# Key products of the cache scores: GpSimd alone, or GpSimd and VectorE in pairs of chunks

## The reference

```
h = rmsnorm(x);  proj = h @ w_in           # 1024 -> 2824: conv, gating, q, k, v, forget logits
logf = log_sigmoid(f + b_f)
prompt: causal attention over 512 tokens, 8 heads of 64, logits + sum of logf
sample: s_past = (q . k_past) * 64**-0.5 + logf + suffix sums of the cached logf
        p = softmax([s_past, s_new]);  o = p @ [v_past, v]
x = x + concat(rmsnorm of the three mixers) @ w_o
x = x + mixture of 32 experts (top 1 group, top 2 in it);  x = x + (p @ w_ple) * sigmoid(...)
```

## Time and profile before

| | us |
|---|---|
| median of three runs | 1118.66 (1113.89 to 1123.4) |
| the profiled execution, its own time | 1116.41 |
| its span | 1114.6 |
| PE busy / DVE busy / ACT busy / POOL busy | 894.7 / 322.5 / 192.6 / 315.8 |
| key products on POOL (L662) x32 | 145.1 |
| key reductions on DVE (L1743) x32 | 72.9 |
| mean granted clock of PE | 0.889 |

### The profile page before, as it was taken

One profiled execution on the slowest core, in us unless ns is written; L12 is line 12 of the kernel. 1 busy time (PEld: TensorE's weight loads), 2 busy tenths in 40 slices (PEclk: granted clock), 3 DMA queues, 4 the chain that ended last, 5 costly groups with the idle time before them and its releaser, 6 DMA issues.

```text
span 1114.6 us, 11569 instructions
## 1 busy us (share of the span) xinstructions
PE 894.7 (80%) x4270; PEld 464.2 (42%) x4270; DVE 322.5 (29%) x710; ACT 192.6 (17%) x388; POOL 315.8 (28%) x336
## 2 busy tenths in 40 slices
PE   2899929998878868767988788778788787886796
PEld 2488716675753424433333333233233333332342
DVE  5217455776464213453100000000000000000562
ACT  2010114554400000211110110110111011100332
POOL 5637899891002231002111111110111111001110
PEclk9899968998869799888998898899889889988799
DMA  9146676662604898640999999999999999998310
GB/s 310 45 151 225 225 253 213 223 226 110 247 1 166 339 376 328 255 179 21 359 413 409 400 412 395 409 414 402 412 416 410 400 411 404 424 401 340 154 40 38
DMA packets 53688, 316.42 MB, mean 284 GB/s; under 512 B 11103, under 2 KB 23967, under 8 KB 32905
## 3 DMA queue, kind: packets, MB, share of 16 engines
q1 hardware_dynamic: 30720, 232.43, 52.1%
q0 software_dynamic: 14512, 76.17, 18.9%
q10 hardware_dynamic: 8416, 7.30, 2.1%
HBM read 309.31 MB, written 14.82 MB: 291 GB/s over the span
## 4 chain that ended last, share of the span: by engine, by line
PE 38%; DMA 36%; POOL 13%; DVE 7%; issue 3%; ACT 2%; SPq 1%; POOLq 0%; DVEq 0%; ACTq 0%
DMA arena<-in_w_up 28%; PE psum L1572 12%; POOL arena L662 9%; PE psum L1680 5%; DMA arena<-in_cache_v,indices 5%; PE psum L1424 4%; PE psum L1277 3%; PE psum L1203 3%; POOL arena L615 2%; DMA arena<-in_w_down 2%; PE psum L1343 2%; DVE arena L1743 1%; POOL arena L593 1%; PE psum L1528 1%; PE psum L1365 1%
## 5 line engine op out<-in xcount | busy, mean ns | idle before, releaser
L1572 PE MATMUL psum<-arena 128*64 128x512 f32 x1024 | 271.6, 691 | 80.7 <-DMA arena<-in_w_up 80.7
L1572 PEld LDWEIGHTS psum<-arena 128*64 128x64 f32 x1024 | 90.7, 158 | 237.5 <-issue 235.4
L662 POOL TENSOR_TENSOR arena<-arena 128x2048 f32<-128x2048 f32 x32 | 145.1, 4535 | 3.6 <-ACTq L824 3.0
L2178 DVE TENSOR_TENSOR arena<-arena,psum 64x512 f32<-64x512 f32 x32 | 22.1, 692 | 382.1 <-ACT arena L1060 382.1
L1587 PE MATMUL psum<-arena 128*64 128x512 f32 x512 | 118.7, 605 | 4.2 <-DMA arena<-in_w_down 3.6
L692 POOL COPY indices<-row_list 128x1 int32 (+1 forms) x26 | 4.7, 181 | 306.0 <-ACT arena L1066 306.0
L1743 DVE TENSOR_REDUCE arena<-arena 128x32 f32<-128x2048 f32 x32 | 72.9, 2283 | 57.3 <-POOL arena L662 57.0
L1203 PE MATMUL psum<-arena 128*128 128x260 f32 x384 | 84.6, 383 | 0.7 <-ACT arena L827 0.7
L1277 PE MATMUL psum<-arena 128*128 128x260 f32 x320 | 79.3, 402 | 0.0
L1203 PEld LDWEIGHTS psum<-arena 128*128 128x128 f32 x384 | 72.8, 190 | 12.3 <-ACT arena L827 1.2
L1060 ACT ACTIVATE arena<-psum 64x512 f32<-64x512 f32 x32 | 18.8, 588 | 332.7 <-PE psum L1572 332.7
(11 more groups left out here) (318 smaller groups left out, 862.6 us busy)
## 6 DMA issues: line engine op xcount, KB each, us to landing
arena<-in_w_down SPq DMA_DIRECT2D x32, 2048.0 KB, 25.1
arena<-in_w_gate SPq DMA_DIRECT2D x31, 2048.0 KB, 18.2
arena<-in_w_up SPq DMA_DIRECT2D x31, 2048.0 KB, 22.6
arena<-in_w_in SPq DMA_DIRECT2D x11, 1024.0 KB
arena<-in_x_prompt SPq DMA_DIRECT2D x8, 512.0 KB, 6.7
arena<-in_w_o SPq DMA_DIRECT2D x1, 4096.0 KB, 14.0
arena<-in_w_ple_gate SPq DMA_DIRECT2D x1, 4096.0 KB, 26.4
arena<-moe_rows SPq DMA_DIRECT2D x4, 1024.0 KB, 7.8
```

What stands on the lines that cost most here:

```text
L662: pool.tensor_tensor(r, r, q_rep, ALU.mult).then_inc(kmul, 1)
L1572: last = mm(bank(s)[m * SLOTS:(m + 1) * SLOTS, :], hgT[s][:, k, :], w_gu[s][m][:, k, :], start=(k == 0), stop=(k == DC - 1))
```

## The change

- **Pairs.** The first 24 key chunks (`SHARED`) are worked in pairs: GpSimd multiplies the even chunk, VectorE the odd one, and VectorE reduces both. VectorE reads the query from PSUM bank 6, where PE leaves it (`qb` is no fill any more). The last eight chunks stay with GpSimd, and their reductions stand in steps 1 to 6 of the attention (`REDUCE_AT`).
- **Six slots.** The ring has six slots for the first 24 chunks; two lie over the normalised rows and the input rows, whose first use afterwards waits for reduction 24. GpSimd issues four gathers ahead of its constants, two after them, and from then on two per pair, two pairs ahead.
- **Forget gate.** PE transposes the forget logits behind the first projected tile, not the fourth; VectorE works the gate in three parts behind pairs 1, 2 and 3, and some of its operands are in PSUM bank 7. ACT's Exp and Ln stand behind the second and the third copy of a projected tile.
- **Scans.** The eight scans stand ahead of the sum of the query's halves.
- **Value copies.** v0 and v1 behind pair 9, v2 and v3 behind pair 10; then pair 11.
- Semaphores are shared or renumbered in the value and expert stages, with constants added to their waits.

```diff
+SHARED = 24
+V_AFTER = {9: (0, 1), 10: (2, 3)}
+REDUCE_AT = {24: (1, 0), 25: (1, 1), 26: (2, 1), 27: (3, 0), 28: (3, 1), 29: (4, 1), 30: (5, 1), 31: (6, 0)}
+SLOT = [n % 6 if n < SHARED else n % 4 for n in range(CHUNKS)] + [n % 4 for n in range(CHUNKS)]
+def arrived(n):
+    return 16 * (1 + SLOT[:n].count(SLOT[n]))
...
-        ring = [at(region_b + s * CW, CW) for s in range(4)]
+        ring = [at(region_b + s * CW, CW) for s in range(4)] + [at(xn0, CW), at(x0, CW)]
-        f_a, f_b, f_c, f_d = (small(TILES, HC) for _ in range(4))
+        f_a, f_c, f_d = (psum[:, 7, n * TILES * HC:(n + 1) * TILES * HC].rearrange("p (t h) -> p t h", h=HC) for n in range(3))
+        f_b, f_e, f_g = (small(TILES, HC) for _ in range(3))
... GpSimd
-            for s in range(3):
-                load_chunk(0, s)
+            for n in range(4):
+                load_chunk(0, n)
...
+            for half in "ab":
+                pool.wait_ge(free_of(f"x{QT}{half}"), AT[f"x{QT}{half}"][1] + 1)
+            load_chunk(0, 4)
+            load_chunk(0, 5)
             pool.wait_ge(qb_ready, 1)
...
-            for n in range(CHUNKS):
-                products(n % 4, 16 * (n // 4 + 1))
-
-                pool.wait_ge(kred, n + 1)
-                if n + 3 < CHUNKS:
-                    load_chunk(0, n + 3)
-                else:
-                    load_chunk(1, n + 3 - CHUNKS)
+            for n in range(0, SHARED, 2):
+                products(n)
+                if n:
+                    pool.wait_ge(kred, n)
+                    load_chunk(0, n + 4)
+                    load_chunk(0, n + 5)
+            for n in range(SHARED, CHUNKS):
+                products(n)
+                if n > SHARED:
+                    pool.wait_ge(kred, n)
+                    load_chunk((n + 3) // CHUNKS, (n + 3) % CHUNKS)
... ScalarE
-            wait_full(act, "qb")
-            act.activation(q_bc, fill("qb"), ACT.Copy).then_inc(free_of("qb"), 1)
-            act.wait_ge(free_of("qb"), AT["qb"][1] + 1)
-            act.nop().then_inc(qb_ready, 1)
+            act.wait_ge(qb_full, 1)
+            act.activation(q_bc, bank(6), ACT.Copy).then_inc(qb_ready, 1)
...
+                if q == 1:
+                    act.wait_ge(f_part, 1)
+                    act.activation(f_b, f_a, ACT.Exp, scale=-1.0).then_inc(f_part, 1)
+                if q == 2:
+                    act.wait_ge(f_part, 3)
+                    act.activation(f_d, f_c, ACT.Ln).then_inc(f_part, 1)
... TensorE
-            pe.wait_ge(f_free, 1)
-            for s in range(2):
-                for q in range(2):
-                    project(s, q, 16, None if s == 0 else q + 1)
...
+            project(0, 0, 16, None)
             wait_free(pe, "f")
+            pe.wait_ge(f_free, 1)
             for t in range(TILES):
...
             done(last, "f")
+            project(0, 1, 16, None)
+            for q in range(2):
+                project(1, q, 16, q + 1)
... VectorE
+            dve.wait_ge(lf_in, 16)
+            for h in range(HC):
+                step(v.tensor_tensor_scan(decay[:, :, h], ones, logf_pages[:, :, h], 0.0, ALU.mult, ALU.add))
+            tell(suf_ready)
             dve.wait_ge(free_of("qs"), AT["qs"][1] + 1)
             v.tensor_tensor(q_s[0:NB, :], q_parts[0:NB, 0, :], q_parts[0:NB, 1, :], ALU.add).then_inc(qs_ready, 1)
...
+            def reduce_keys(n):
+                if n >= SHARED:
+                    dve.wait_ge(kmul, SHARED // 2 + n - SHARED + 1)
+                elif n % 2 == 0:
+                    dve.wait_ge(kmul, n // 2 + 1)
+                v.tensor_reduce(scores[:, n * KEYS * HC:(n + 1) * KEYS * HC], ring[SLOT[n]].rearrange("p (a d) -> p a d", d=HD),
+                                AX.X, ALU.add).then_inc(kred, 1)
+            q_rep = bank(6).rearrange("p (o n) -> p o n", o=1).to_broadcast([P, KEYS, WC])
+            def key_pair(n):
+                dve.wait_ge(kv_in[SLOT[2 * n + 1]], arrived(2 * n + 1))
+                r = ring[SLOT[2 * n + 1]].rearrange("p (k n) -> p k n", k=KEYS)
+                step(v.tensor_tensor(r, r, q_rep, ALU.mult))
+                reduce_keys(2 * n)
+                reduce_keys(2 * n + 1)
...
+            dve.wait_ge(qb_ready, 1)
+            key_pair(0)
+            key_pair(1)
+            forget_in()
+            key_pair(2)
+            forget_exp()
+            key_pair(3)
+            forget_log()
+            key_pair(4)
+            mask_ws()
+            for n in range(5, SHARED // 2):
+                key_pair(n)
+                for t in V_AFTER.get(n, ()):
+                    copy_values(t)
```

More of the change, by code:

```diff
@@ L78 @@
 FILLS = (["params"] + [f"x{t}{s}" for t in range(TILES) for s in "ab"]
-         + ["qs", "qb", "f", "ws", "ks", "vs", "ct"] + [f"{n}{t}" for t in range(QT) for n in "kv"]
+         + ["qs", "f", "ws", "ks", "vs", "ct"] + [f"{n}{t}" for t in range(QT) for n in "kv"]
          + ["suffix"]
@@ L1185, in _ @@
                 if s:
-                    wait_free(pe, "qb")
                     pe.wait_ge(qs_ready, 1)
                     pe.wait_ge(consts_built, 2)
-                    done(mm(fill("qb"), row_sel[0:NB, :], q_s[0:NB, :], start=True, stop=True), "qb")
+                    mm(bank(6), row_sel[0:NB, :], q_s[0:NB, :], start=True, stop=True).then_inc(qb_full, 1)
                 for k in range(DC):
@@ L1748, in _ @@
+            tell(suf_ready)
             dve.wait_ge(free_of("qs"), AT["qs"][1] + 1)
             v.tensor_tensor(q_s[0:NB, :], q_parts[0:NB, 0, :], q_parts[0:NB, 1, :], ALU.add).then_inc(qs_ready, 1)
-            for j in range(2):
-                reduce_static(j)
-            wait_full(dve, "f")
-            dve.wait_ge(consts_in, 16 * 15)
-            step(v.tensor_tensor(f_nat[:, 0:QT, :], fill("f")[:, 0:QT * HC].rearrange("p (t h) -> p t h", h=HC), outer(bf_bc, QT), ALU.add))
-            step(v.tensor_tensor(f_nat[0:NB, QT, :], fill("f")[0:NB, QT * HC:TILES * HC], bf_bc[0:NB, :], ALU.add))
@@ L1776, in _ @@
-            step(v.scalar_tensor_tensor(out=f_nat, in0=f_nat, scalar=0.0, in1=f_d, op0=ALU.min, op1=ALU.subtract))
-            tell(logf_ready)
-            for j in range(2, 6):
-                reduce_static(j)
-            dve.wait_ge(lf_in, 16)
-            for h in range(HC):
-                ins = v.tensor_tensor_scan(decay[:, :, h], ones, logf_pages[:, :, h], 0.0, ALU.mult, ALU.add)
-                step(ins)
-            tell(suf_ready)
-            for j in range(6, EARLY):
-                reduce_static(j)
@@ L1789, in _ @@
-            for t in range(QT):
+            def reduce_keys(n):
[6 more added lines that the diff above has]
+            q_rep = bank(6).rearrange("p (o n) -> p o n", o=1).to_broadcast([P, KEYS, WC])
@@ new lines, in key_pair, with forget_in @@
+            def key_pair(n):
[4 more added lines that the diff above has]
+                reduce_keys(2 * n + 1)
+            def forget_in():
+                wait_full(dve, "f")
+                dve.wait_ge(consts_in, 16 * 15)
+                step(v.tensor_tensor(f_nat[:, 0:QT, :], fill("f")[:, 0:QT * HC].rearrange("p (t h) -> p t h", h=HC), outer(bf_bc, QT), ALU.add))
+                step(v.tensor_tensor(f_nat[0:NB, QT, :], fill("f")[0:NB, QT * HC:TILES * HC], bf_bc[0:NB, :], ALU.add))
+                dve.nop().then_inc(free_of("f"), 1)
+                step(v.tensor_scalar(f_a, f_nat, -1.0, None, ALU.mult))
+                step(v.tensor_tensor(f_a, f_nat, f_a, ALU.max))
+                tell(f_part)
@@ new lines, in forget_exp, with forget_log @@
+            def forget_exp():
+                dve.wait_ge(f_part, 2)
+                step(v.tensor_scalar(f_c, f_b, 1.0, None, ALU.add))
+                step(v.tensor_scalar(f_e, f_c, -1.0, None, ALU.add))
+                tell(f_part)
+            def forget_log():
+                dve.wait_ge(f_part, 4)
+                step(v.tensor_scalar(f_c, f_e, 0.0, None, ALU.is_equal))
+                step(v.tensor_tensor(f_e, f_e, f_c, ALU.add))
+                step(v.reciprocal(f_e, f_e))
+                step(v.tensor_tensor(f_d, f_d, f_b, ALU.mult))
+                step(v.tensor_tensor(f_d, f_d, f_e, ALU.mult))
+                step(v.tensor_tensor(f_g, f_c, f_b, ALU.mult))
+                step(v.tensor_tensor(f_d, f_d, f_g, ALU.add))
+                step(v.scalar_tensor_tensor(out=f_nat, in0=f_nat, scalar=0.0, in1=f_d, op0=ALU.min, op1=ALU.subtract))
+                tell(logf_ready)
@@ L1882, in _ @@
                     layer_norms()
-            assert done == CHUNKS
             dve.wait_ge(half_free, rest_halves - 4)
```

87 lines of the change are left out of this document (32 added, 55 removed).

## The result

The kernel with the change takes 1112.0 us (median of 16 runs, 1108.2 to 1117.1), the kernel before beside it 1118.0 (16 runs): ratio 0.995, 95% interval 0.993 to 0.997. The forecast was 1105, 11.3 us less; the medians differ by 6.0 us. 1112.0 lies inside the stated range of 1097 to 1119, but only about half of the forecast saving is there. The profiled execution took 1110.66 us against 1116.41 before, so it shows a difference of the measured size, 5.75 us, and the two traces can be set against each other.

The account below looks back on a forecast made before the run. Key products were taken to bound the kernel before 168 us, PE from 168 to 255, VectorE at 255 to 270. 1116.4 - 6.3 (start) - 3.5 - 1.5 (both step 12) = 1105.1 us; range 1097 to 1119.

Parts of the forecast that it names:

- The pair: Key chunks before attention: VectorE's product 2.3 us, a pair of chunks 6.9 us with a step's wait.
- held by GpSimd's product: Rival: VectorE's product waits for GpSimd's, a pair up to 9.1 us, time 1111; chance 0.12 together with slow pairs.
- The head: Start of the kernel: a fourth gather delays the first product from 43.84 to 45.1; net +0.6 us for PE.
- V0 and the diagonal: From v0's copy at 141.5 to attention's start: diagonal at 161.1 instead of 167.44, minus 6.3 us.
- DMA: Gathers and weights during the pairs: 7.7 us a pair at 339 GB/s, the next limit, covered by VectorE's wait.
- late-weights rival: Denser gathers delay PE's weight groups, adding each excess over 14 us to v0, time up to 1129; chance 0.09.
- Step 12: Late in attention: no reduction there, so PE waits 3.5 us less, and the slow matmuls behind save 1.5.
- Eight chunks instead of fifteen: nothing: Attention's steps 1 to 6: the eight remaining chunks delay reductions by 1 or 2 us without stopping PE, cost nothing.
- As long as before within 2 us: From attention's end to the end of the span: later stages move as a block, their length unchanged within 2 us.

Follow-up runs that it names:

- q_sbuf: The changed kernel with VectorE's product reading the query from its SBUF copy instead of PSUM; 1118.8 us, 1.002 of the kernel before.
- reduce_late: The changed kernel with the eight late reductions spread over steps 1 to 11 of attention; 1109.4 us, 0.993 of the kernel before.
- r_after: The changed kernel run again, unchanged, for a second trace; 1114.2 us, 0.997 of the kernel before.
- r_before: The kernel before run again, unchanged, for a second trace; ratio 1.001.
- the second set: The repeated runs of both kernels, unchanged: the kernel before 1.001, the changed kernel 0.997 (1114.2 us).
- v_last: The changed kernel with all four value copies behind pair 11; 1102.3 us, 0.988 of the kernel before.
- v_paced: The changed kernel with value copies behind pair 11, late reductions spread, and gathers held back to the projections' pace; 1105.7 us, 0.990 of the kernel before.
- both edits: The changed kernel with value copies behind pair 11 and late reductions spread over steps 1 to 11; 1098.6 and 1097.4 us, 0.984 and 0.982.
- v_eight_r: Value copies behind pair 11, late reductions spread, and eight distinct semaphores for GpSimd's DMAs, run six times; 1093.6 us, 0.978 of the kernel before.

## Why the prediction was wrong

**The pair, right.** Product 2.28 against 2.3, pair 6.7 against 6.9, GpSimd's product unchanged; q_sbuf shows that the rival "held by GpSimd's product" is real with the query in SBUF and is what the PSUM bank avoids.

**The head, right in kind.** The scans took 3.6 us in their hole, as priced. The first product came at 43.3, not 45.1: the broadcast behind GpSimd's constants began only 0.3 us later than before, at 41.36, for the 1.3 that the fourth gather had been priced at, and ran 1.29 us where it had taken 2.04. But the start of the projections varies between executions of one kernel by more than that: it lies between 46.7 and 49.7 us in the six traces with the old head (mean 48.4) and between 47.6 and 50.0 in the fourteen with the new one (mean 49.1). The means differ by 0.7 us, close to the forecast +0.6.

**V0 and the diagonal, a little too small, and the first pair of traces flatters it.** In them v0 stands at 138.8 instead of 141.4 and the diagonal moves by minus 9.4 instead of minus 6.3. But the kernel before had its latest start of all there (projections from 49.7, diagonal at 167.4) and the change its earliest. Against the mean of all six traces with the old start, 166.1, the two of the change (158.0, 158.8) are 7.7 us earlier.

**DMA.** It had been put at 7.7 us a pair and was not the bound; 361 GB/s passed, not 339, and with two pairs of gathers ahead a pair took 6.7. The late-weights rival had 0.09 and a condition on every execution; it is a matter of single executions, two of eleven, at 4.0 and 6.3 us.

**Step 12, the size right by luck, the reason not.** The wait fell by 2.2 us of the forecast 3.5, and all 2.9 us behind it are saved where 1.5 were taken: 5.1 against 5.0, two misses that cancel. The reason given was that no reduction stands there any more. In reduce_late one does, and the gap is 1.14 us. What reduce_late lacks against the kernel before is the wait of 1.48 us for GpSimd's product and the reduction ahead of step 11's inversion; which of the two made the gap was not tried.

**"Eight chunks instead of fifteen: nothing", wrong.** Up to step 6 there are eight reductions, as there had been before, but closer together: behind the inversion of step 2 and in both places of step 3, three places in a row, where before the change one stood behind the negation of each step and only step 3 had a second. The forecast counted them against a step's length and not against their places. PE's wait at step 4 went from 0.73 to 0.48 + 1.92 us, and sixteen matmuls from 2.37 to 3.99: 3.3 us lost. Which of the eight does it was not tried; spread, attention took 119.0 us, 6.4 less than before, of which the forecast had 5.0; as built it took 2.8 less.

**"As long as before within 2 us", wrong, and this is the step that failed.** The sum to the end of attention was minus 11.3; the first pair of traces has minus 12.2 and all traces together minus 10.5, by an earlier start and a loss at step 4 that nearly cancel. But 3.1 us of it go to GpSimd's closing drain, in every trace with the change's semaphores (9.27 us instead of 6.16). The prediction named renumbered counters and held that they cost nothing; which semaphores the DMAs of GpSimd count on is what set it. The 3.3 us behind the values in the profiled execution are no part of the change: from the last value product to the embedding it is 37.9 or 41.2 us with either start (37.9 in before and r_after, 41.1 in r_before, 41.2 in after). That the profiled pair differed by the same 5.75 us as the medians is therefore chance: the earliest start against the latest, less the slow form of this stretch.

**What stays open.** Six traces of kernels with the old start end attention at 290.0 to 292.8 us (mean 291.3), the two of the change at 280.6 and 280.9: 10.5 us less, 7.4 after the drain. The medians gave 6.0 and 3.0. So of the 5.3 us that the first medians lack against the forecast, the drain is 3.1, the start and attention 0.8, and 1.4 stay open, 4.4 in the second set. Late weights in some executions go the right way and would give some 0.9 us on average at the rate above (10.3 us in eleven traces); both profiled executions of the change were also faster than their medians, by 1.3 and 7.3 us, those of the kernel before by 1.6 and 2.2. Another stretch varies too: from the first to the last product with cached values it is 90.3 to 91.0 us in before, r_before, after and r_after, but 93.5 to 93.9 in the other four with the old start and 94.1 and 94.7 in the two with late weights. How often either kernel has it long is not known. The difference was not traced to a place. For the versions run several times the same sum comes closer: v_last 15.1 against 15.0, reduce_late 5.5 (with its late weights) against 7.9, v_paced 12.6 against 11.9; both edits 22.4 less at the end of attention and 3.1 back, 19.3, against medians 18.9 and 20.5 lower; v_eight_r 23.5 and 1.9 more at the end, 25.4, against 25.1. These use one or two traces each, so a match within 1 us is partly chance. Why the drain depends on which semaphores are shared is open too; only that it does is shown.

## What to carry to other kernels

When an engine is relieved, look at how long it then idles and move the work behind that idle time ahead of it: 20 us of VectorE's idling held two pairs, worth 9 us at the diagonal, about as much as the change itself had brought there. Fewer instructions of a kind can still cost more where they stand back to back in a full schedule: place them by what each step leaves free. And read the last microseconds of both traces: a stage that the edit doesn't touch can change by 3 us through shared bookkeeping. Where two kernels differ by half a per cent, compare each stage over several traces: the first pair alone put 1.7 us too much on the start and 3.3 us on a stretch that varies by itself.

## What was not expected of the hardware

- GpSimd's closing drain takes 1.75, 6.0, 6.2 or 9.3 us by the semaphores that its DMAs count on, the same to 10 ns in all traces of kernels with the same semaphores.
- A gather's issue on GpSimd was stretched from 0.96 to 2.84 us beside a VectorE product with both inputs in SBUF.
- PE's matmuls behind the values ran at a mean granted clock of 0.83 or 0.55 over 10 us with the same instructions around them, worth 3.3 us between one execution and another.
- The start of PE's projections varied by 3 us between executions of kernels with the same start (46.7 to 49.7).
